# A causal mask moved into the free rows of a decay product, filled by GpSimd

## The chip, the core and the metric

One core of a Trainium2 chip. The metric is the time of one execution of the whole program in microseconds of device time: the median of three runs, and beside it one profiled execution. Throughout, TensorE runs at a granted clock of 1.00, its upper level of 2.4 GHz.

## What is computed

A block of a hybrid model over 512 tokens of width 1024 and a second block behind it. What matters here is the gated delta rule in the first block, in chunks. In the reference:

```python
G = jnp.cumsum(gc, axis=-1)
tri = jnp.tril(jnp.ones((C, C), dtype=bool))
strict = jnp.tril(jnp.ones((C, C), dtype=bool), -1)
gamma = jnp.exp(jnp.where(tri, G[..., :, None] - G[..., None, :], -jnp.inf))
kb = kc * bc[..., None]
A = jnp.where(strict, jnp.einsum("bnhid,bnhjd->bnhij", kb, kc) * gamma, 0.0)
T = lax.linalg.triangular_solve(A + eye, ...)
```

For each of 8 heads the keys' products with themselves are multiplied by decays that are 0 above the diagonal, and the triangular matrix that results is inverted. The kernel uses chunks of 128 tokens, four for each head.

## The kernel before

All weights come as panels of 128 output columns by 1024 (512 KB). SyncE loads a panel into one of two buffers (`conv_load`, L1289), ScalarE makes its rounded half (`split_hi`, L344), VectorE the rest (`split_lo`, L355), and TensorE forms 24 products of 128x512 with it (L552, L553, L555). Engines run their own lists of work, tied by semaphores. In this first stage each list goes through steps m, one panel each: panels 1 to 8 are keys, 9 to 16 queries, 17 to 24 values, 25 and on gates. ScalarE and VectorE split panel m + 2 in step m once they have caught up.

The decays of the keys. After panel 12 has its fourth slice, TensorE turns a small table of logarithms into 8 rows of 512 (`rows_turned(0)`), which ScalarE (`rows_hi`, L1530) and VectorE (`rows_lo`, L1534) write, as a rounded part and a rest, into partitions 0 to 7 and 32 to 39 of `rowsR`, row 0. The other 112 partitions hold zeros from a memset by GpSimd (L2966). `selR` (L1567, ScalarE, from `sel`, which VectorE forms at L1672 in its step m = 2) holds for each head ones in the two partitions of that head. In steps m = 12 to 15, two heads a step, TensorE spreads a head's row over 128 partitions (L1503), adds the causal mask by a second product, identity by `maskTb` in bf16 (L1504), and forms the keys' products (L1507). ScalarE takes the exponential with a bias for each row (L1617), VectorE multiplies the two (L1719) into `aA`. The queries' decays go the same way in steps 20 to 23 with `rowsR`, row 2, and their own masking product (L1477).

SyncE writes each head's `aA` to `scr_a` in DRAM (L1301, `g_a`), behind the loads of panels 16 and 18; behind the load of panel 19 it waits for all eight, reads the 32x32 blocks of the diagonal back (L1307, `d_u`) and goes on to panel 20. VectorE inverts these blocks in small steps between m = 18 and 26 (`solve`, L1273 and L1276). Behind panel 29 SyncE writes the inverse to `scr_t` (L1312, `d_w`), and reads it back head by head (L1325). From 218 us TensorE combines the blocks (`gdn_pe`, L1822 and on).

GpSimd's list in this stage is: memsets, part of the first norm and of the splitting of `x` (`first_pool`), the copies of the index keys (`key_copies`, L1446, for TensorE's L1489 behind panel 8), and then 13 times a transfer of 1 MB from DRAM to DRAM (`copy_quarter`, L928) and one that adds 1 MB to it (`add_sum`, L936), for weight sums that the feed-forward layers read hundreds of microseconds later. Sum i is issued when all moves before it have landed, and the next copy right behind it; before the eighth sum GpSimd also waits for `d_u`. Then come the level masks (`gdn_pool`, L1778), which wait for `d_w`.

Of the kernel before, what the change touches and what calls it, by code (L numbers as in the profile page):

```python
# [19 lines left out]
F32 = mybir.dt.float32  # L20
# [3 lines left out]
ACT = mybir.ActivationFunctionType  # L24
ALU = mybir.AluOpType
AX = mybir.AxisListType.X

P = 128
T = 512
NB = T // P  # L30
# [5 lines left out]
GH = 8  # L36
# [3 lines left out]
NEG = -1.0e30  # L40
# [79 lines left out]
for _name, _c in VEC:  # L120
# [2 lines left out]
NV = _n  # L123

MATS = ["ident", "ones", "lastrow", "blk64", "ropesel", "maskT", "zero0", "zero1", "zero2", "maskS", "hot",
        "lev5", "lev6"]
MO = {m: i for i, m in enumerate(MATS)}


# [35 lines left out]
def build(nc, I, out):  # L165
    with ExitStack() as ctx:
# [19 lines left out]
        identb, maskTb = (sb(n, [P, P], BF16) for n in ("identb", "maskTb"))  # L186
# [48 lines left out]
        def rep(ap, n):  # L235

            return ap.unsqueeze(1).broadcast_to([ap.shape[0], n, ap.shape[1]])
# [1197 lines left out]
        def first_pool(pool):  # L1435
            late_pool(pool, "norm1")
            for t in range(1, DT, 2):
                pool.wait_ge(n_hi, t + 1)
                pool.wait_ge(x_ready, t)
                pool.tensor_tensor(xl[:, t, :], x_scaled[:, t, :], xh[:, t, :].bitcast(F32), ALU.subtract).then_inc(x_ready, 1)  # L1440
# [8 lines left out]
        def conv_pe(pe):  # L1449
# [14 lines left out]
            for m in range(4, ZGA + ALONE):  # L1464
# [33 lines left out]
                if 12 <= m < 16:  # L1498
                    pe.wait_ge(g_rl, 1)
                    for s in range(2):  # L1500
                        hd, row, dots = 2 * (m - 12) + s, pb[4 + 2 * s][:, :], pb[5 + 2 * s]
                        wait(pe, g_e1, hd - 1)
                        pe.matmul(row, selR[:, hd, :], rowsR[:, 0, :], start=True, stop=False)  # L1503
                        pe.matmul(row, identb[:, :], rep(maskTb[:, :], NB), start=False, stop=True).then_inc(g_r1, 1)  # L1504
                        wait(pe, g_a, hd - 1)
                        for b in range(NB):
                            t = pe.matmul(dots[:, B(b)], kF[:, hd, B(b)], kF[:, hd, B(b)], start=True, stop=True)  # L1507
                        t.then_inc(g_kk, 1)
# [16 lines left out]
        sel = coef[:, 1, 0:GH]  # L1525

        def rows_hi(act, r):
            act.wait_ge(g_cr, 1 + r)
            act.wait_ge(s_set, 5)
            act.activation(rowsR[0:8, 2 * r, :], pb[6][0:8, :], ACT.Copy).then_inc(g_rh, 1)  # L1530

        def rows_lo(dve, r):
# [4 lines left out]
        def conv_act(act):  # L1537
            first_act(act)
            for m in range(2, ZGA + ALONE):
# [22 lines left out]
                if m == 4:  # L1562
                    act.wait_ge(s_mats, 32)
                    act.activation(identb[:, :], ident, ACT.Copy).then_inc(s_maskb, 1)
                    act.activation(maskTb[:, :], M("maskT"), ACT.Copy).then_inc(s_maskb, 1)
                    act.wait_ge(g_sel, 1)
                    act.activation(selR[:, :, :], sel.unsqueeze(2).broadcast_to([P, GH, P]), ACT.Copy).then_inc(g_sel, 1)  # L1567
                for c in {9: [4, 5], 10: [6, 7]}.get(m, TURN.get(m, [m - 3] if 11 <= m < 27 else [])):
                    hd, bank = c % 8, pb[2 + c % 2]
                    act.wait_ge(g_tr, c + 1)  # L1570
# [62 lines left out]
        def gate_dve(dve, n):  # L1633

            t, second = gate_tile(n)
            if second:
                dve.wait_ge(out_free, n + 1)
                dve.tensor_tensor(kF[:, t, :], kF[:, t, :], gtmp[t % 2], ALU.mult).then_inc(g_gm, 1)

        def conv_dve(dve):  # L1640
            first_dve(dve)
            for m in range(ZGA + ALONE):
# [71 lines left out]
                if 12 <= m < 16:  # L1714
                    for s in range(2):
                        hd = 2 * (m - 12) + s
                        dve.wait_ge(g_e1, hd + 1)
                        dve.wait_ge(g_kk, hd + 1)
                        dve.tensor_tensor(aA[:, hd, :], pb[5 + 2 * s][:, :], aA[:, hd, :], ALU.mult).then_inc(g_a, 1)  # L1719
                if 20 <= m < 24:  # L1720
                    for s in range(2):
                        hd = 2 * (m - 20) + s
# [1236 lines left out]
        def _(pool):  # L2959
# [2 lines left out]
            pool.memset(epsc[:, 1:2], 128.0 * EPS).then_inc(s_set, 1)  # L2962
            pool.memset(zeros, 0.0).then_inc(g_zero, 1)
            pool.memset(inv32, 0.0).then_inc(s_set, 1)
            for r in (0, 2):
                pool.memset(rowsR[:, r, :].bitcast(F32), 0.0).then_inc(s_set, 1)  # L2966
            pool.wait_ge(s_set, 3)
            pool.memset(yb[:, 2:4, :].rearrange("p a b -> p (a b)")[:, 0:1024:33], 1.0).then_inc(g_w0, 1)
            first_pool(pool)
            key_copies(pool)  # L2970
            copy_quarter(pool, 0, s_sums)
            for i in range(EARLY):
# [615 lines left out]
def _matrices():  # L3588
    i, j = np.arange(P)[:, None], np.arange(P)[None, :]
    out = np.zeros((P, len(MATS), P), np.float32)  # L3590
    out[:, MO["ident"]] = i == j
    out[:, MO["ones"]] = 1.0
    out[:, MO["lastrow"]] = (i == P - 1) * np.ones_like(j)
    out[:, MO["blk64"]] = (i // 64 == j // 64) / 64.0
    r = (j - 64) % 32
    out[:, MO["ropesel"]] = (j >= 64) & (i % 32 == r)
    out[:, MO["maskT"]] = np.where(j < i, NEG, 0.0)
    out[:, MO["maskS"]] = np.where(j > i, NEG, 0.0)
    out[:, MO["hot"]] = (i >= 64) & (i % 32 == j) & (j < 16)
    for l in (5, 6):  # L3600
        b = 1 << l
        out[:, MO[f"lev{l}"]] = (i // (2 * b) == j // (2 * b)) & (i // b % 2 == 0) & (j // b % 2 == 1)
    return out
# [102 lines left out]
```

## Time and profile before

| | us |
|---|---|
| median of three runs | 2117.58 (2115.51 to 2117.63) |
| profiled execution | 2118.94 |
| its span | 2117.1 |
| TensorE busy | 2096.8 (99%) |
| VectorE busy | 1495.1 (71%) |
| ScalarE busy | 1101.9 (52%) |
| GpSimd busy | 561.7 (27%) |

The profile's page gives the busy time of each engine and the costliest instructions; the views below it give waits, the chain of work that ended last, and each engine's instructions in order of time. TensorE's matmuls are pipelined: one lasts 0.39 us in the records, but the next starts 0.23 us after it. The stage of the change is the first 220 us.

### The profile page before, as it was taken

Reading aid. Unit: us, or ns where it says so; the run is one execution under the profiler, and the core shown is the slowest. Engines: PE = TensorE matmul, PEld = TensorE weight load, DVE = VectorE, ACT = ScalarE, POOL = GpSimd, SP = SyncE. Lnnn points to the kernel's source line nnn. Section 1 sums busy time; section 2 is a strip of 40 time slices with the busy share of each in tenths; the row PEclk is TensorE's granted clock in tenths of the full one; section 3 lists DMA queues with packets and bytes.
Section 4 is the critical chain, followed back from the end, with each engine's and each line's share of the span. In section 5 each row is a group of like instructions: output and inputs, shape, how many; then the busy total and the mean of one; then the engine's idle time right before and its main releaser. Section 6 shows DMA issues by size and latency. Waiting matters only on the chain.

```text
span 2117.1 us, 32333 instructions
## 1 busy us (share of the span) xinstructions
PE 2096.8 (99%) x12060; PEld 1821.4 (86%) x12060; DVE 1495.1 (71%) x2428; ACT 1101.9 (52%) x1928; POOL 561.7 (27%) x475
## 2 busy tenths in 40 slices
PE   9999999999999999999999999999999999999998
PEld 6887898888888889888887899999887778999897
DVE  6878334777467686876777687877566875868775
ACT  5877433435444354453776454554445764544543
POOL 2100531243333110153774231101322222311012
PEclk9999999999999999999999999999999999999999
DMA  7997212446676565644845559887653235555663
GB/s 258 247 262 204 94 59 70 152 167 210 236 202 179 152 185 169 157 122 129 298 164 173 140 195 260 259 258 230 159 157 89 79 91 153 170 189 180 209 190 129
DMA packets 148348, 372.01 MB, mean 176 GB/s; under 512 B 39008, under 2 KB 43360, under 8 KB 132832
## 3 DMA queue, kind: packets, MB, share of 16 engines
q1 hardware_dynamic: 129600, 241.49, 33.9%
q0 software_dynamic: 10448, 76.55, 17.2%
q10 hardware_dynamic: 8144, 51.91, 6.9%
q8 instruction: 96, 1.57, 0.3%
q14 instruction: 60, 0.49, 0.1%
HBM read 356.78 MB, written 132.64 MB: 231 GB/s over the span
## 4 chain that ended last, share of the span: by engine, by line
PE 87%; DVE 5%; ACT 2%; DMA 2%; issue 1%; DVEq 1%; POOLq 0%; SPq 0%; POOL 0%; ACTq 0%
PE bank L430 8%; PE bank L431 8%; PE bank L434 8%; PE bank L552 6%; PE bank L555 6%; PE bank L553 6%; PE bank L998 5%; PE bank L1002 5%; PE bank L1000 5%; PE bank L449 4%; PE bank L448 4%; PE bank L447 4%; PE bank L2538 2%; PE bank L1798 1%; PE bank L2566 1%
## 5 line engine op out<-in xcount | busy, mean ns | idle before, releaser
L344 ACT ACTIVATE b_wh<-b_raw 128x1024 fp32r<-128x1024 f32 (+1 forms) x312 | 321.8, 1034 | 533.0 <-PE bank L434 245.7
L355 DVE TENSOR_TENSOR b_wl<-b_raw,b_wh 128x1024 fp32r<-128x1024 f32 (+2 forms) x269 | 338.8, 1262 | 110.3 <-ACT b_wh L344 107.2
L552 PE MATMUL bank<-b_xh,b_wh 128*128 128x512 f32 x712 | 294.6, 414 | 0.6 <-DVE b_wl L355 0.6
L553 PE MATMUL bank<-b_xl,b_wh 128*128 128x512 f32 x712 | 278.2, 391 | 0.0
L555 PE MATMUL bank<-b_xh,b_wl 128*128 128x512 f32 x704 | 275.9, 392 | 0.0
L1206 POOL TENSOR_TENSOR b_yl<-b_arena,b_yh 128x512 fp32r<-128x512 f32 x42 | 65.2, 1553 | 537.3 <-ACT b_yh L1117 342.6
L430 PE MATMUL bank<-b_xh,b_wh 128*128 128x512 f32 x504 | 196.9, 391 | 0.0
L431 PE MATMUL bank<-b_xl,b_wh 128*128 128x512 f32 x504 | 196.1, 389 | 0.0
L434 PE MATMUL bank<-b_xh,b_wl 128*128 128x512 f32 x496 | 193.1, 389 | 0.0
L355 POOL TENSOR_TENSOR b_wl<-b_raw,b_wh 128x1024 fp32r<-128x1024 f32 (+1 forms) x45 | 103.9, 2310 | 226.1 <-ACT b_wh L344 188.4
L555 PEld LDWEIGHTS bank<-b_xh,b_wl 128*128 128x128 f32 x704 | 132.1, 188 | 29.1
L552 PEld LDWEIGHTS bank<-b_xh,b_wh 128*128 128x128 f32 x712 | 134.2, 188 | 24.9 <-DVE b_wl L355 1.3
L553 PEld LDWEIGHTS bank<-b_xl,b_wh 128*128 128x128 f32 x712 | 134.4, 189 | 21.2 <-issue 0.2
L998 PE MATMUL bank<-b_seven_hi,b_more_wh 128*128 128x256 f32 x512 | 145.0, 283 | 0.0
L1002 PE MATMUL bank<-b_seven_hi,b_more_wl 128*128 128x256 f32 x512 | 144.9, 283 | 0.0
L1000 PE MATMUL bank<-b_seven_lo,b_more_wh 128*128 128x256 f32 x512 | 144.9, 283 | 0.0
L355 DVE TENSOR_TENSOR b_more_wl<-b_more_raw,b_more_wh 128x1024 fp32r<-128x1024 f32 x92 | 120.0, 1305 | 32.1 <-ACT b_more_wh L344 29.8
L998 PE MATMUL bank<-b_seven_hi,b_wh 128*128 128x256 f32 x496 | 140.6, 283 | 0.4 <-DVE b_wl L355 0.4
L1000 PE MATMUL bank<-b_seven_lo,b_wh 128*128 128x256 f32 x496 | 140.4, 283 | 0.0
L1002 PE MATMUL bank<-b_seven_hi,b_wl 128*128 128x256 f32 x496 | 140.3, 283 | 0.0
L344 ACT ACTIVATE b_more_wh<-b_more_raw 128x1024 fp32r<-128x1024 f32 x92 | 96.4, 1053 | 46.5 <-PE bank L449 19.8
L430 PEld LDWEIGHTS bank<-b_xh,b_wh 128*128 128x128 f32 x504 | 94.6, 188 | 19.3
(576 smaller groups left out, 5539.8 us busy)
## 6 DMA issues: line engine op xcount, KB each, us to landing
scr_sums<-in_quarters POOLq DMA_DIRECT2D x37, 1024.0 KB, 9.8
scr_sums<-in_quarters ACTq DMA_DIRECT2D x35, 1024.0 KB, 5.2
b_raw<-scr_sums SPq DMA_DIRECT2D x110, 256.0 KB, 3.3
b_more_raw<-scr_sums SPq DMA_DIRECT2D x108, 256.0 KB, 3.2
scr_sums<-scr_sums POOLq DMA_DIRECT2D x24, 1024.0 KB, 8.5
b_raw<-in_quarters SPq DMA_DIRECT2D x92, 256.0 KB, 3.0
b_more_raw<-in_quarters SPq DMA_DIRECT2D x76, 256.0 KB, 3.1
scr_sums<-in_quarters ACTq DMA_DIRECT2D x8, 1536.0 KB, 8.8
```

Of the source, the lines that this page charges most:

```text
L344: act.activation(panel_hi_lo(n)[0][:, cols], raw_of(n)[:, cols], ACT.Copy).then_inc(w_hi, 1)
L355: dve.tensor_tensor(lo, raw_of(n)[:, cols], hi.bitcast(F32), ALU.subtract).then_inc(w_lo, 1)
L430: pe.matmul(bank[:, :], ph[:, w], hi[:, x, :], start=(k == 0), stop=False)
L431: last = pe.matmul(bank[:, :], ph[:, w], lo[:, x, :], start=False, stop=(n in SIDE_BY_SIDE and k == kt - 1))
L434: last = pe.matmul(bank[:, :], pl[:, w], hi[:, x, :], start=False, stop=(k == kt - 1))
L447: pe.matmul(bank, hi, ph, start=start, stop=False, skip_group_check=more)
L552: pe.matmul(bank[:, :], ph[:, w], hi[:, x, :], start=(k == 0), stop=False)
L553: last = pe.matmul(bank[:, :], ph[:, w], lo[:, x, :], start=False, stop=(n in SIDE_BY_SIDE and k == kt - 1))
L555: last = pe.matmul(bank[:, :], pl[:, w], hi[:, x, :], start=False, stop=(k == kt - 1))
L998: pe.matmul(bank, ph[:, w], xs_hi[i][:, k, :], start=(i < 4 and k == 0), stop=False, skip_group_check=(i > 3))
L1000: pe.matmul(bank, ph[:, w], xs_lo[i][:, k, :], start=False, stop=False, skip_group_check=(i > 3))
L1002: m = pe.matmul(bank, pl[:, w], xs_hi[i][:, k, :], start=False, stop=(k == 3), skip_group_check=(i > 3))
```

## The change

The mask goes into the first product. New constant matrices are loaded with the others: `barrier` holds, in each of the free 112 partitions but one, -1e30 in the columns before some place a, and `reach` ones from a on. Their product is -1e30 or less where a column lies before a row with a place between. The places are 1 to 127 without every eighth (4, 12, ...), as 111 fit; the entries that these leave unmasked lie beside the diagonal at the middle of a group of eight columns, and VectorE bounds the exponentials by 1e15 before it multiplies. GpSimd copies `barrier` into row 0 of `rowsR` (128x512, in place of a memset) and adds `reach` to the spread `sel` for `selR` (128x1024, in place of ScalarE's fill). Both stand behind `first_pool` and ahead of `key_copies`, behind a wait for the constants and one for `g_sel`, 1. ScalarE's `rows_hi` now waits for `g_sel`, 2.

```diff
-MATS = [..., "lev5", "lev6"]
+MATS = [..., "lev5", "lev6", "barrier", "reach"]
@@ conv_pe, 12 <= m < 16
-                        pe.matmul(row, selR[:, hd, :], rowsR[:, 0, :], start=True, stop=False)
-                        pe.matmul(row, identb[:, :], rep(maskTb[:, :], NB), start=False, stop=True).then_inc(g_r1, 1)
+                        pe.matmul(row, selR[:, hd, :], rowsR[:, 0, :], start=True, stop=True).then_inc(g_r1, 1)
@@ rows_hi
             act.wait_ge(s_set, 5)
+            act.wait_ge(g_sel, 2)
@@ conv_act, m == 4
-                    act.wait_ge(g_sel, 1)
-                    act.activation(selR[:, :, :], sel.unsqueeze(2).broadcast_to([P, GH, P]), ACT.Copy).then_inc(g_sel, 1)
@@ conv_dve, 12 <= m < 16
-                        dve.tensor_tensor(aA[:, hd, :], pb[5 + 2 * s][:, :], aA[:, hd, :], ALU.mult).then_inc(g_a, 1)
+                        dve.scalar_tensor_tensor(out=aA[:, hd, :], in0=aA[:, hd, :], scalar=GAMMA_MAX, in1=pb[5 + 2 * s][:, :],
+                                                 op0=ALU.min, op1=ALU.mult).then_inc(g_a, 1)
@@ gpsimd
-            for r in (0, 2):
-                pool.memset(rowsR[:, r, :].bitcast(F32), 0.0).then_inc(s_set, 1)
+            pool.memset(rowsR[:, 2, :].bitcast(F32), 0.0).then_inc(s_set, 1)
             ...
             first_pool(pool)
+            pool.wait_ge(s_mats, 32)
+            pool.wait_ge(g_sel, 1)
+            pool.tensor_copy(blk(rowsR[:, 0, :]), rep(M("barrier"), NB)).then_inc(s_set, 1)
+            pool.tensor_tensor(selR[:, :, :], bc(sel, P), rep(M("reach"), GH), ALU.add).then_inc(g_sel, 1)
             key_copies(pool)
@@ _matrices
+    free = [r for r in range(P) if not (r < GH or 32 <= r < 32 + GH)]
+    for r, a in zip(free, [a for a in range(1, P) if a % 8 != 4]):
+        out[r, MO["barrier"]] = NEG * (np.arange(P) < a)
+        out[r, MO["reach"]] = np.arange(P) >= a
```

## Rows read from the trace of the kernel before

**Rows 1.** Busy time by stretch: length, five engines, TensorE clock, DMA share, GB/s.

```profile
130.00:150.00 20.00, 20.00 (x98) 16.55 (x97) 14.15 (x21) 11.67 (x35) 2.68 (x4) 1.00 0.90 227
150.00:210.00 60.00, 57.46 (x294) 46.29 (x293) 53.34 (x103) 46.06 (x96) 4.84 (x7) 1.00 0.77 215
```

**Rows 2.** Waits of TensorE, 30 to 420 us: total us, times, longest us.

```profile
PE bank L1521 <- DVE b_arena L1735: 1.9, 3, 0.7
...
PE bank L1822 <- DMA b_arena<-scr_t: 0.2, 1, 0.2
```

**Rows 3.** Chain of waits in order of time: start us, us, what. Last masked pair.

```profile
119.62 0.23 PE bank L1503
119.85 0.23 PE bank L1504
```

**Rows 4.** Chain of waits, same columns: the transfer of panel 21.

```profile
136.77 8.89 DMA b_raw<-in_gv
```

**Rows 5.** VectorE L1719 and L1428: count, ns min/median/max, first and last start, shapes.

```profile
L1719 DVE TENSOR_TENSOR b_gdn_a<-bank,b_gdn_a x8: 690/692/693, 99.3 to 125.5; 128x512 f32<-128x512 f32 x8
L1428 DVE SCALAR_TENSOR_TENSOR b_arena<-b_h,b_arena,bank x8: 739/742/748, 21.4 to 28.5; 128x512 f32<-128x512 f32 x8
```

**Rows 6.** Order of ScalarE: start us, us, instruction, idle before and its releaser.

```profile
44.91 1.06 ACT L1567 ACTIVATE b_gdn_sel<-b_coef 128x1024 fp32r<-128x1024 f32 x1
46.38 1.06 ACT L344 ACTIVATE b_wh<-b_raw 128x1024 fp32r<-128x1024 f32 x1 [0.41 <-PE bank L555]
```

**Rows 7.** Order of VectorE: the row of `sel`.

```profile
44.72 0.16 DVE L1672 TENSOR_TENSOR b_coef<-b_mats 128x8 f32<-128x8 f32 x1
```

**Rows 8.** Order of GpSimd: key copies, first copy and first sum of quarters.

```profile
32.02 1.36 POOL L1446 COPY b_rrow<-b_arena 64x512 f32<-64x512 f32 x2 [0.45 <-DVE b_arena L1668]
34.04 0.76 POOL L928 DMA_DIRECT2D scr_sums<-in_quarters  x1 [0.66 <-issue]
40.05 0.88 POOL L936 DMA_DIRECT2D scr_sums<-in_quarters  x1 [5.25 <-DMA scr_sums<-in_quarters]
```

**Rows 9.** GpSimd L1778, a product with a repeated matrix (columns as rows 5).

```profile
L1778 POOL TENSOR_TENSOR b_arena<-b_gdn_a,b_mats x16: 1264/1282/2251, 213.3 to 300.1; 128x512 f32<-128x512 f32 x16
```

**Rows 10.** Order of GpSimd: seventh, eighth and thirteenth sum, then the level masks.

```profile
112.85 0.81 POOL L936 DMA_DIRECT2D scr_sums<-scr_sums  x1 [12.16 <-DMA scr_sums<-in_quarters]
...
134.97 0.81 POOL L936 DMA_DIRECT2D scr_sums<-scr_sums  x1 [20.77 <-DMA b_gdn_y<-scr_a]
...
197.87 0.81 POOL L936 DMA_DIRECT2D scr_sums<-in_quarters  x1 [9.56 <-DMA scr_sums<-in_quarters]
...
213.35 5.99 POOL L1778 TENSOR_TENSOR b_arena<-b_gdn_a,b_mats 128x512 f32<-128x512 f32 x4 [14.67 <-DMA scr_t<-b_gdn_y]
```

**Rows 11.** Order of SyncE's issues: blocks read back, then panels 20 and following.

```profile
129.68 2.34 SPq L1307 DMA_DIRECT2D b_gdn_y<-scr_a  x4
132.07 25.65 SPq L1289 DMA_DIRECT2D b_raw<-in_gv  x5
```

**Rows 12.** Writes to `scr_a` at 116 to 118 and 124.5 to 127 us, with landing.

```profile
L1301 SPq DMA_DIRECT2D scr_a<-b_gdn_a x2: 326/326/327, 116.5 to 117.6; - x2
DMA to landing us min/median/max: 9.0/9.1/9.2
...
L1301 SPq DMA_DIRECT2D scr_a<-b_gdn_a x2: 319/320/320, 125.2 to 126.2; - x2
DMA to landing us min/median/max: 2.0/2.7/3.5
```

**Rows 13.** Order of VectorE: split of panel 20, then the solver's first step.

```profile
141.46 1.21 DVE L355 TENSOR_TENSOR b_wl<-b_raw,b_wh 128x1024 fp32r<-128x1024 f32 x1
...
142.82 0.18 DVE L1273 TENSOR_TENSOR b_gdn_y<-b_gdn_y 128x31 f32<-128x31 f32 x1
```

**Rows 14.** Order of TensorE: first product of panel 20.

```profile
144.83 0.48 PE L552 MATMUL bank<-b_xh,b_wh 128*128 128x512 f32 x1
```

**Rows 15.** Writes to `scr_t`, with landing.

```profile
L1312 SPq DMA_DIRECT2D scr_t<-b_gdn_y x4: 326/590/620, 208.8 to 210.4; - x4
DMA to landing us min/median/max: 2.1/2.6/2.7
```

More of the change, by code:

```diff
@@ L125 @@
 MATS = ["ident", "ones", "lastrow", "blk64", "ropesel", "maskT", "zero0", "zero1", "zero2", "maskS", "hot",
-        "lev5", "lev6"]
+        "lev5", "lev6", "barrier", "reach"]
 MO = {m: i for i, m in enumerate(MATS)}
@@ L1638, in gate_dve @@
                 dve.tensor_tensor(kF[:, t, :], kF[:, t, :], gtmp[t % 2], ALU.mult).then_inc(g_gm, 1)
+        GAMMA_MAX = 1.0e15
         def conv_dve(dve):
```

## The prediction

> **What bounds the kernel now.** I read the busy time by stretch first. Between 130 and 150 us TensorE is busy all 20.00 us; between 150 and 210 us it is busy 57.46 of 60, and VectorE 53.34 [rows 1]. So before 150 us only TensorE's own work counts, and after it VectorE comes close to being the bound. The waits say the same: TensorE waits three times, 1.9 us in all, for VectorE's L1735, and once, 0.2 us, for the copy of `scr_t` [rows 2]. Then the chain of waits, followed in order of time: the products at 92 to 132 us stand on it one behind the other, and each of the eight masking products L1504 holds it for 0.23 us just as each L1503 does; the last pair is shown [rows 3]. From 132 us it goes through VectorE, a panel's transfer that took 8.89 us [rows 4], ScalarE, and then VectorE nearly alone to 208 us. The last view is the order of GpSimd's instructions and the time from issue to landing of the transfers beside them, because the change puts a wait into GpSimd's queue.
>
> **TensorE.** The change removes eight L1504 products, one a head. Each holds the chain for 0.23 us [rows 3]: 8 x 0.23 = 1.8 us, all in a stretch in which TensorE is the bound. L1503 stays, its free rows filled with the mask at no columns more. The whole saving is there by 119.9 us, where the last of them stands.
>
> **VectorE.** Eight L1719 multiplications become a minimum and a multiplication in one instruction. L1719 takes 692 ns; the same kind of instruction, one operand in PSUM, takes 742 ns at L1428 [rows 5]. 8 x 0.05 = 0.4 us. Before 130 us TensorE doesn't wait for this result (the product is read by SyncE and by later work), so I take 0, with 0.4 as the other end.
>
> **ScalarE.** The fill of `selR`, 1.06 us, goes. The next split started after 0.41 us of waiting for TensorE [rows 6]: it will only wait longer. Worth 0. The new wait in `rows_hi` is for a fill that ends 40 us earlier: 0.
>
> **GpSimd, the fills.** They stand after the first norm and before the key copies. They need `g_sel`, which VectorE raises at its L1672, at 44.72 us plus 0.16 [rows 7]. In the kernel before GpSimd was at the key copies by 32.02 us [rows 8]. The copy of the barrier rows is a 512-element copy as L1446 is, 1.36 us for two [rows 8], so 0.7; the upper end is L1778's 1.28 [rows 9]. The sum for `selR` is 1024 elements: twice L1778's 1282 ns [rows 9], 2.6 us; with nothing lower at hand than twice the 0.68 of a copy, the bounds are 1.4 and 2.6, and I take 2.4 as the kind of instruction is L1778's. The fills end near 44.9 + 0.7 + 2.4 = 48.0 (47.0 to 48.8). The key copies end 1.4 us later, near 49.4. TensorE wants them behind panel 8, while VectorE at 44.72 us is in its step m = 2, six steps earlier: 0. The memset that goes stood ahead of the norm, on an idle engine: 0. The constants grow by 128 KB; their first reader here is ScalarE just ahead of its 44.91, which shows no wait [rows 6]: 0.
>
> **GpSimd, what is queued behind the wait.** Behind it stand not only the key copies, but the transfers of `copy_quarter` and `add_sum`: 13 copies and 13 sums of 1 MB, each sum waiting for the moves before it. From the start of the key copies to the first issue it took 34.04 - 32.02 = 2.0 us [rows 8], so that issue comes at 50.0 instead of 34.04: 16 us later (15 to 16.8). The first sum then waited for the first copy until 40.05, 6.0 us. From the first sum at 40.05 to the seventh at 112.85 are six steps of 12.1 us [rows 8, 10]; the seventh moves to 56.0 + 72.8 = 128.8. Its partner, the copy issued 0.5 us later, needs about one step: it would end near 141 instead of 125.
>
> In the kernel before, that is the quiet stretch. GpSimd waits there, 20.77 us in all, for the blocks read from `scr_a`, and moves nothing from about 125 to 134.97 us [rows 10]. In it SyncE writes the last two heads to `scr_a`, reads the blocks back from 129.68 us, and behind these, in the same queue, issues the load of panel 20 at 132.07 [rows 11]. With GpSimd's transfers under way two writes to `scr_a` took 9.0 and 9.2 us; without them 2.0 and 3.5 [rows 12]. A loaded panel took 8.89 us [rows 4]. So the delayed chain meets just these.
>
> Here is what they may cost. The blocks are needed by the first L1273 at 142.82 - 1.8 = 141.0 [rows 13]. Issued from 127.9 to 130.2 (129.68 and 2.34 us of issuing, less 1.8) and landing like the loaded writes 9.1 us after the last issue, they land near 139.3: in time by 1.7 us. If the writes before them land late as well, by up to 9.2 - 3.5 = 5.7 us, they are 4 us late. Panel 20, issued at 132.07 - 1.8 = 130.3 and loaded, lands at 139.2; its two splits take 1.06 [rows 6] and about 1.2 us, so it is ready at 141.5. TensorE starts on it at 144.83 - 1.8 = 143.0 [rows 14]. Cover: 1.5 us; with the 5.7 of the writes ahead of it in the queue the cost is 4.2. The two delays run side by side and are not added. Bounds 0 and 4.2. The writes at 123.4 and 124.4 fall into the end of one GpSimd pair (116 to 128.5), so I take a third, 1.5 us. It can't be hidden after 150 us, where VectorE follows without a gap.
>
> The chain of sums then goes on: the eighth starts near 142 instead of 134.97, and the thirteenth, 62.9 us later [rows 10], at 205 instead of 197.87. Taking a step, it ends near 216. The inverse is written to `scr_t` from 208.80 us, four transfers landing 2.1 to 2.7 us after issue [rows 15]: now beside the last sum. By the ratio of [rows 12], 9.1 to 2.75, they would land 6 us later; the lower bound is 0, if the sum is through by then. TensorE has no cover there: it already waits for this copy at 218 us [rows 2], and so does GpSimd at 213.35 [rows 10]. I take 1.8, a third of the upper end: only one of GpSimd's transfers is left then, not a pair as in [rows 12].
>
> **The sum.** -1.8 (TensorE) + 0 + 0 + 1.5 (blocks and panel 20) + 1.8 (`scr_t`) = +1.5 us. The profiled execution took 2118.94 us, 2117.1 of it span: 2120.4. It is 1.4 us above the median of the runs shown, 2117.58, so against those the forecast is 2119.1.
>
> **The rivals**, on the scale of the median.
> 1. The saving is kept: the queues share the DMA engines in turn, and a short transfer beside a long one takes twice its time, not three times. Then the blocks land at 130.2 + 2 x 2.75 = 135.7, panel 20 no later than 139.2, both inside their cover, and the writes to `scr_t` lose 2.7 us at most, of which a last sum that ends early takes the rest. 2117.6 - 1.8 = 2115.8. For it: TensorE is busy all 20.00 us at 130 to 150 us, so nothing there is late now [rows 1]. Against it: the loaded writes took 9.1 us where the others took 2.75 [rows 12], and at 213 us there is no cover. The Trainium skill, DMA: Bandwidth & Descriptors, section "Queues, rings and completion order", has the rule behind this rival: each DMA engine goes round between the queues that have work, a packet from each. By that rule the time would be this rival's; the trace agrees that both queues move on side by side, but not with twice.
> 2. Slower. GpSimd's wait for `g_sel` sets the order of the transfers, and both meetings cost their upper ends: -1.8 + 4.2 + 6 = +8.4, 2126; it decides from the point at which the writes to `scr_a` end more than 1.5 us late, panel 20's cover. With one of them at its end, +4.2 to +5, 2122. For it: transfers fill 0.90 of the engines' time at 130 to 150 us [rows 1]. [...]
> 3. Faster than the saving. With GpSimd's transfers elsewhere the panel that took 8.89 us lands early, VectorE's run of work starts up to 0.9 us earlier (ScalarE split it at 136.77 + 8.89 = 145.7, while TensorE had left panel 19 by 144.83 [rows 4, 14]), and of the 1.9 us of waits behind it some go too: -1.8 - 0.9 to -1.8 - 1.9, about 2114.
> 4. The change does nothing for the end: VectorE's run from 150 us takes the 1.8 us back as waits of TensorE. It needs VectorE's run to start at its old time, which hangs on the panel of 8.89 us. 2117.6, inside the forecast's own range.
>
> **How the numbers follow.** The forecast and rival 4 hold 0.48 (2116.5 to 2121.8), rival 1 0.26, rival 2 0.21, rival 3 0.05. About 0.2%, 4.2 us, is what a measurement of this kernel can tell from no change. Faster by more than that needs rival 3 and more: 0.02. Slower by more is most of rival 2 and a little of the forecast: 0.22. The rest, 0.76, is the same. The range reaches from 2114.8 (rival 1 and a microsecond) to 2124.5 (half of rival 2).
>
> **What would show it.** Of the profile after: L1504 gone and TensorE's stretch at 92 to 127 us shorter by 1.8; GpSimd's first `copy_quarter` near 50 us; its seventh sum near 129, with no wait of 20 us behind it; the reads of `scr_a` landing after 137 instead of before 135; new or longer waits of TensorE at 143 to 165 (L552, L1515, L1521) and at L1822; the last sum near 205. If the seventh sum is near 113 as before, my reading of the wait is wrong, and everything after the first line falls with it. If the transfers move but the landings don't lengthen, rival 1 holds.

## The result and the profile after

| | before | after |
|---|---|---|
| median | 2116.89 us (2115.51 to 2117.63) | 2130.78 us (2127.62 to 2131.45) |
| ratio to before, 95% interval | | 1.0062 (1.0050 to 1.0073) |
| span of the profiled execution | 2117.1 us | 2128.9 us |

The kernel became slower: the medians lie 13.9 us apart, and the ratio is 1.0062. The forecast was 2119.1, 1.5 us over the kernel before, and its range ended at 2124.5. In the kernel after, some of the lines behind L1503 have moved by one or two: L1506 and on are the products of the keys, L1514 and L1520 stand for L1515 and L1521, L1779 for L1778, L1823 for L1822.

First the waits of TensorE, 100 to 260 us (us in total, times, the longest; those of 0.5 us and less are left out):

```profile
PE bank L1823 <- DMA b_arena<-scr_t: 7.1, 1, 7.1
PE bank L1454 <- ACT b_arena L1559: 4.8, 1, 4.8
PE bank L1460 <- DVE b_arena L1710: 1.8, 1, 1.8
PE bank L1520 <- DVE b_arena L1736: 1.2, 2, 0.7
```

In place of 1.9 + 0.2 us [rows 2] there are 14.9 us, and three of the waits are large: two at the turn to panel 20 and one at the copy of `scr_t`. The busy time by stretch (columns as rows 1) shows them with their clock, with the last stretch of the kernel before ahead of the three of the kernel after:

```profile
210.00:230.00 20.00, 19.47 (x117) 16.47 (x116) 8.35 (x7) 10.59 (x15) 15.23 (x11) 1.00 0.66 182
...
130.00:150.00 20.00, 13.40 (x59) 10.38 (x58) 8.85 (x15) 5.79 (x21) 1.35 (x2) 0.84 0.98 269
150.00:210.00 60.00, 58.03 (x297) 47.05 (x295) 54.26 (x98) 48.50 (x101) 6.72 (x10) 1.00 0.84 234
210.00:230.00 20.00, 12.92 (x58) 10.66 (x57) 6.97 (x12) 4.97 (x6) 6.66 (x5) 0.89 0.86 200
```

From 130 to 150 us TensorE was busy 20.00 of 20 us [rows 1], now 13.40; from 210 to 230 us it was busy 19.47, now 12.92. Between the two stretches nothing changed (58.03 of 60 against 57.46). The loss has two places, 75 us apart.

GpSimd's order shows the delay (start us, us, instruction, idle before and releaser; these columns hold for all orders below):

```profile
42.75 1.06 POOL L2972 CAST b_gdn_rows<-b_mats 128x512 fp32r<-128x512 f32 x1 [13.45 <-DVE b_coef L1672]
43.77 2.34 POOL L2973 TENSOR_TENSOR b_gdn_sel<-b_coef,b_mats 128x1024 fp32r<-128x1024 f32 x1
...
48.82 0.76 POOL L928 DMA_DIRECT2D scr_sums<-in_quarters  x1 [0.66 <-issue]
...
124.03 0.81 POOL L936 DMA_DIRECT2D scr_sums<-in_quarters  x1 [14.30 <-DMA scr_sums<-in_quarters]
...
137.39 0.81 POOL L936 DMA_DIRECT2D scr_sums<-scr_sums  x1 [12.02 <-DMA scr_sums<-in_quarters]
...
152.59 0.81 POOL L936 DMA_DIRECT2D scr_sums<-scr_sums  x1 [13.85 <-DMA scr_sums<-in_quarters]
...
212.31 0.81 POOL L936 DMA_DIRECT2D scr_sums<-in_quarters  x1 [10.39 <-DMA scr_sums<-in_quarters]
224.15 5.91 POOL L1779 TENSOR_TENSOR b_arena<-b_gdn_a,b_mats 128x512 f32<-128x512 f32 x4 [11.02 <-DMA scr_t<-b_gdn_y]
```

GpSimd idles 13.45 us for VectorE's `sel` and issues its first 1 MB copy at 48.82 instead of 34.04 us [rows 8]. The rows at 124.03, 137.39 and 152.59 are the sixth, seventh and eighth sum. The seventh stood at 112.85 before and the thirteenth at 197.87 [rows 10]; now they stand at 137.39 and 212.31. The quiet stretch before the eighth sum, 20.77 us of waiting for the blocks [rows 10], is gone: it now waits 13.85 us for its own chain.

SyncE's order has what the prediction did not foresee:

```profile
122.88 0.58 SPq L1289 DMA_DIRECT2D b_raw<-in_gv  x1
126.02 11.45 SPq L1307 DMA_DIRECT2D b_gdn_y<-scr_a  x4
137.52 23.87 SPq L1289 DMA_DIRECT2D b_raw<-in_gv  x5
...
212.50 9.11 SPq L1312 DMA_DIRECT2D scr_t<-b_gdn_y  x4
```

The four issues that read the blocks took SyncE 2.34 us [rows 11] and now take 11.45; the four writes of the inverse, which were begun from 208.8 to 210.4 us and took 0.62 us at most [rows 15], now take 9.11 in all. The single issues of the two lines (count, ns min/median/max, first and last start):

```profile
L1307 SPq DMA_DIRECT2D b_gdn_y<-scr_a x4: 322/1412/8171, 126.0 to 135.4; - x4
...
DMA to landing us min/median/max: 4.0/10.4/11.7
...
L1312 SPq DMA_DIRECT2D scr_t<-b_gdn_y x4: 326/590/7477, 212.5 to 214.1; - x4
...
DMA to landing us min/median/max: 2.5/9.4/9.8
```

So not only do the small transfers land late (10.4 and 9.4 us in the median). SyncE itself stands for 8.17 and 7.48 us at one issue, and what is queued behind it, panel 20 the first time, starts that much later. The chain of work that ended last shows it too (start us, us, what). It runs through the four issues at L1307, then through the load of panel 21, which SyncE issues right behind panel 20's, and at the second place through the last write of the inverse:

```profile
127.17 8.17 SPq L1307
...
135.38 2.09 SPq L1307
...
138.12 11.21 DMA b_raw<-in_gv
...
214.14 9.84 DMA scr_t<-b_gdn_y
```

ScalarE's order (a row of before first, then two of after) and TensorE's show the arrival:

```profile
138.38 1.06 ACT L344 ACTIVATE b_wh<-b_raw 128x1024 fp32r<-128x1024 f32 x1 [3.33 <-PE bank L555]
...
143.22 1.06 ACT L344 ACTIVATE b_wh<-b_raw 128x1024 fp32r<-128x1024 f32 x1 [12.28 <-DMA b_raw<-in_gv]
144.18 0.61 ACT L1559 ACTIVATE b_arena<-b_arena 128x512 f32<-128x512 f32 x1
```

```profile
144.85 1.11 PE L1454 MATMUL bank<-b_mats,b_arena 128*128 128x128 f32 x4 [4.78 <-ACT b_arena L1559]
147.78 1.02 PE L1460 MATMUL bank<-b_mats,b_arena 128*8 128x128 f32 x4 [1.82 <-DVE b_arena L1710]
148.45 0.78 PE L552 MATMUL bank<-b_xh,b_wh 128*128 128x512 f32 x1
...
150.89 0.40 PE L552 MATMUL bank<-b_xh,b_wh 128*128 128x512 f32 x1
...
228.57 1.94 PE L1823 MATMUL bank<-b_mats,b_arena 128*128 128x128 f32 x8 [7.08 <-DMA b_arena<-scr_t]
```

ScalarE had the split of panel 20 (L344) at 138.38 before, after 3.33 us of waiting for TensorE. Now it waits 12.28 us for the transfer, and L1559, which TensorE's L1454 needs, stands behind it in the same list. After the pause the same product L552 takes 0.78 us and 2.4 us later 0.40 again: the granted clock of 140 to 150 us is 0.69 in the mean, the lower of the two levels, 1.2 GHz, in a part of it. TensorE had been idle for 4.78 us before that. Behind the second wait the pattern repeats (0.78 at 230.16, and 0.78 is also the clock of 220 to 230 us).

**Where 13.9 us come from.** TensorE starts on panel 2 at 23.60 us in the profile of before and at 20.8 to 23.5 in the others, also where the code up to there is the same (20.80 in e2, 21.89 in e7). So I count each event of TensorE from there. The turn to panel 19 is the start of the four small products L1454 ahead of it. The third row is the first L1515 (now L1514), which stands behind the products of panel 20; below I call it step 20. All columns are of one profiled execution each.

| us after the start of panel 2 | before | after | difference |
|---|---|---|---|
| turn to panel 19 | 114.53 | 112.67 | -1.86 |
| L1515 (now L1514) of step 20 | 127.34 | 134.01 | +6.67 |
| start of L1822 (now L1823) | 194.40 | 207.24 | +12.84 |
| the rest, to the end of the span | 2093.50 | 2107.57 | +14.07 |

To panel 19 the saving is there in full. From there to step 20, over the turn to panel 20, 8.5 us are lost: 4.78 + 1.82 of waits, the rest the lower clock and what follows. The second meeting shows its whole wait, 7.08 against 0.17, less 0.7 us that the stretch between gave back; another 1.2 us go behind it, where the clock is at the lower level again.

### The profile page after: what moved, and what is told of

It reads as the page before. It is cut to its first block, busy times and chain, and to the rows that moved or that the text cites. A ratio compares the mean times of both kernels' runs of the same rounds, so it can differ in the third digit from the quotient of the medians.

```text
span 2128.9 us, 32318 instructions
## 1 busy us (share of the span) xinstructions
PE 2098.2 (99%) x12052; PEld 1823.1 (86%) x12052; DVE 1495.9 (70%) x2428; ACT 1101.3 (52%) x1927; POOL 567.3 (27%) x476
## 4 chain that ended last, share of the span: by engine, by line
PE 87%; DVE 5%; ACT 3%; DMA 2%; issue 1%; DVEq 1%; SPq 1%; POOLq 0%; POOL 0%; ACTq 0%
PE bank L430 8%; PE bank L431 8%; PE bank L434 8%; PE bank L552 6%; PE bank L555 6%; PE bank L553 6%; PE bank L998 5%; PE bank L1000 5%; PE bank L1002 5%; PE bank L449 4%; PE bank L448 4%; PE bank L447 4%; PE bank L2539 2%; PE bank L1799 1%; PE bank L2567 1%
## 5 line engine op out<-in xcount | busy, mean ns | idle before, releaser
L344 ACT ACTIVATE b_wh<-b_raw 128x1024 fp32r<-128x1024 f32 (+1 forms) x312 | 321.8, 1034 | 556.0 <-PE bank L434 231.3
L552 PE MATMUL bank<-b_xh,b_wh 128*128 128x512 f32 x712 | 295.7, 415 | 0.7 <-DVE b_wl L355 0.6
L552 PEld LDWEIGHTS bank<-b_xh,b_wh 128*128 128x128 f32 x712 | 134.7, 189 | 25.1 <-DVE b_wl L355 1.3
L344 ACT ACTIVATE b_more_wh<-b_more_raw 128x1024 fp32r<-128x1024 f32 x92 | 96.4, 1054 | 44.7 <-PE bank L449 19.8
```

The costliest lines, as they stand in the source:

```text
L344: act.activation(panel_hi_lo(n)[0][:, cols], raw_of(n)[:, cols], ACT.Copy).then_inc(w_hi, 1)
L552: pe.matmul(bank[:, :], ph[:, w], hi[:, x, :], start=(k == 0), stop=False)
```

## The experiments

The theory: GpSimd's 1 MB transfers, 15 us late, are in flight while SyncE issues its small ones for `scr_a` and `scr_t`; they hold up SyncE's issuing, and all three large waits follow. The rivals: the new instructions cost something themselves (the fills, the minimum), the late start costs in another way and the meeting is only a companion, or the saving of 1.8 us doesn't exist. The edits below are against the kernel after, where nothing else is said. "First meeting" is L1307 with the two waits at panel 20, "second meeting" is L1312 with the wait at L1823.

**e1, the fills between the first sums.** GpSimd does all it did, but sends its first copy and first sum off before it waits for `sel`.

```diff
-            pool.wait_ge(s_mats, 32)
-            pool.wait_ge(g_sel, 1)
-            pool.tensor_copy(blk(rowsR[:, 0, :]), rep(M("barrier"), NB)).then_inc(s_set, 1)
-            pool.tensor_tensor(selR[:, :, :], bc(sel, P), rep(M("reach"), GH), ALU.add).then_inc(g_sel, 1)
...
             for i in range(EARLY):
+                if i == 1:
+                    pool.wait_ge(s_mats, 32)
+                    pool.wait_ge(g_sel, 1)
+                    pool.tensor_copy(...)
+                    pool.tensor_tensor(...)
```

> The changed kernel, but GpSimd's wait for g_sel and its two fills stand between the first and the second sum of the quarters, where it waits some 10 us for a transfer anyway. Theory (the harm is only that the transfers behind the wait start 15 us late): the first copy is issued near 34 us again, the eighth sum waits about 20 us for the blocks, SyncE's four issues of the blocks take 2.3 us together and not 11.5, and the saving of the eight products is left: 1.8 us faster than the kernel before, about 2115. Rival (the fills, the larger constants or the two-step operation on VectorE cost the time): it stays near 2131.

Measured: 2114.19 us beside 2117.85 for before, ratio 0.9987 (0.9978 to 0.9996). The first copy is issued at 31.59 us, the issues at L1307 and the landings are:

```profile
L1307 SPq DMA_DIRECT2D b_gdn_y<-scr_a x4: 322/566/778, 128.4 to 130.2; - x4
...
DMA to landing us min/median/max: 2.4/2.9/3.0
```

No issue is held (0.78 us at most), L1312 takes 2.26 us, and TensorE's large waits are gone (L1823 0.7 us in all). The products, the minimum and the fills are all there, and the whole loss is gone. So the loss lies in the place of the wait and the fills, and none of it in what the new instructions cost.

**e2, the wait alone.** The kernel before, with the two waits and nothing else of the change.

```diff
             first_pool(pool)
+            pool.wait_ge(s_mats, 32)
+            pool.wait_ge(g_sel, 1)
             key_copies(pool)
```

> The kernel before with one addition: GpSimd waits for the constants and for g_sel ahead of the key copies; no fill, no new matrix, all products kept. Theory: the whole loss without the saving, 13.9 + 1.8 = 15.7 us slower than the kernel before, near 2132.6; the waits of TensorE behind step m = 17 (about 6.6 us) and at the copy of scr_t (about 7) are there. The fills of 3.4 us are missing from the delay (12.6 us instead of 16), so one of the two meetings may be weaker. Rival: no change against before.

Measured: 2125.84 us, ratio 1.0043 (1.0030 to 1.0055), 8.0 us over before and half of the 15.7 expected. GpSimd's order, SyncE's order and the waits of TensorE:

```profile
42.29 2.00 POOL L1446 COPY b_rrow<-b_arena 64x512 f32<-64x512 f32 x2 [13.51 <-DVE b_coef L1672]
...
127.75 0.81 POOL L936 DMA_DIRECT2D scr_sums<-scr_sums  x1 [13.07 <-DMA scr_sums<-in_quarters]
```

```profile
128.61 9.93 SPq L1307 DMA_DIRECT2D b_gdn_y<-scr_a  x4
```

```profile
PE bank L1454 <- ACT b_arena L1559: 3.3, 1, 3.3
PE bank L1460 <- DVE b_arena L1710: 2.3, 1, 2.3
PE bank L1822 <- DMA b_arena<-scr_t: 1.3, 1, 1.3
```

The first meeting comes with the wait: a pair is issued at 127.75, a microsecond before SyncE's reads, one of which is held for 6.63 us. The second does not come. The first copy goes out at 44.95 instead of 48.82 us, the steps between the sums are 12.7 us long instead of 13.1, and the last sum stands at 202.76 instead of 212.31; L1312 follows at 213.31, 10.5 us behind it, and takes 2.25 us. The wait alone makes some 8 us. That the fills behind it bring the second meeting on top fits this, but no run changes their time alone.

**e3, the pause one sum earlier.** GpSimd's wait for the blocks, which stands ahead of the eighth sum, is put ahead of the seventh.

```diff
-EARLY, FIRST_EARLY = 13, 7
+EARLY, FIRST_EARLY = 13, 6
```

> The changed kernel with GpSimd's wait for the blocks moved one sum forward (ahead of the seventh instead of the eighth), so that the late chain is quiet again while the blocks are read. Theory: SyncE's issues of the blocks take about 2.3 to 4 us, TensorE's waits of 4.8 and 1.8 us near 142 to 148 us and its slow clock behind them go, 8 us are won back; the wait at the copy of scr_t stays or grows, as the last sum is still late (near 206): about 2122. Rival (it is bandwidth over the whole stretch, not this meeting): under 3 us won.

Measured: 2128.57 us, ratio 1.0056 (1.0040 to 1.0071). The meeting was not kept away. The sixth sum, at 125.06 us, was the one that met the reads; L1307 took 9.67 us, one issue 6.24. I had counted the sums by the steps of 12.1 us of before, and they are longer here. The second meeting had another form: L1312 took 3.23 us at 209.84, its writes landing in 3.0 to 3.9 us, but the last sum at 213.00 came ahead of the reads of `scr_t`, and L1823 still waited 5.1 us. The run says only that a pause behind the meeting does not help.

**e4, the pauses at both places.** As e3, and the last sum waits for the inverse's writes (`d_w`).

```diff
+                if i == EARLY - 1:
+                    pool.wait_ge(d_w, 16 * NB)
```

> As the one before, and the thirteenth sum also waits until the inverse is written to scr_t. Theory: both meetings are gone though the transfers are still late: TensorE's wait for the copy of scr_t falls from 7.1 us to under 1, and the time is that of the saving alone, about 2115 to 2117. Rival (the late transfers cost through something else): over 2122.

Measured: 2128.81 us, ratio 1.0060 (1.0047 to 1.0072). Here L1307 was clean (2.43 us at 134.06), but not by the edit: up to the last sum this is the program of e3. In e3's execution the panel's load issued at 106.28 us landed after 5.6 us; in this one, the load issued at 106.33, behind a pair of 105.60, took 13.83 us. ScalarE, the last heads' `aA` and the blocks all came later; step 20 came 130.73 us after the start of panel 2, only 3.3 us earlier than in the kernel after. Which transfers meet can thus differ between executions of one program, and a profile shows one of them. The last sum, now at 215.53, stood in front of the reads of `scr_t` and a panel's load, and TensorE got a new wait:

```profile
PE bank L1842 <- ACT b_gdn_y L1894: 5.5, 1, 5.5
PE bank L1454 <- ACT b_h L1559: 2.4, 2, 1.3
PE bank L552 <- DVE b_wl L355: 1.6, 2, 1.5
```

L1823 now waits 1.3 us in all, but what that gains goes again behind it. The cost was moved, not removed, and the run says nothing of the time without meetings.

**e5, panel 20 ahead of the blocks.** SyncE reads the blocks behind panel 20's load, not ahead of it.

```diff
-                if n == 19:
+                if n == 20:
```

> The changed kernel, but SyncE issues the load of panel 20 ahead of reading the blocks back, so that it no longer stands behind their issues. Theory A (what hurts at 142 us is that the panel is stuck in SyncE's queue behind an issue that itself takes 8 us): TensorE's wait of 4.8 us behind step m = 19 goes, the blocks still land late (near 145) and hold VectorE's solver some 3 us; 3 to 6 us faster than the changed kernel. Theory B (bandwidth: the panel is as late wherever it is issued): within 1 us of it, 2130.8.

Measured: 2126.19 us, ratio 1.0037 (1.0024 to 1.0051). L1307 takes 11.93 us all the same, two of its issues 4.23 and 5.64. Panel 20's load, now issued at 126.97 us ahead of them, lands after 10.7 us, and the wait of 4.8 us at its turn is gone; of the other, at L1460, 1.6 us stay. What stands behind the held issues is late instead: panel 21's load is issued at 139.39 and takes 8.85 us, and TensorE waits 3.0 us at L1454 one turn later, 1.5 at L1514, and 5.4 at L1823. Against the kernel after some 5 us come back by the ratios (1.0037 against 1.0062) and 3.4 us in the profiles, so panel 20's place in the queue was a part of the price, and no more than a part.

**e6, half the delay.** The key copies and the first copy of a quarter go ahead of the wait; the first sum still stands behind the fills.

```diff
+            key_copies(pool)
+            copy_quarter(pool, 0, s_sums)
             pool.wait_ge(s_mats, 32)
...
-            key_copies(pool)
-            copy_quarter(pool, 0, s_sums)
```

> The changed kernel with the key copies and the first copy of quarters ahead of GpSimd's wait and fills: the first sum comes near 48 instead of 55.7 (before: 40.1), half of the delay. Theory (each meeting is a matter of phase): the seventh sum's partner ends near 133, so the blocks meet only its tail, and the last sum ends near 210, so scr_t meets its tail; 2 to 8 us slower than before, 2119 to 2125. Rival (any delay costs the same): 2131. Rival (bandwidth in proportion): +7, 2124.

Measured: 2121.51 us, ratio 1.0017 (1.0007 to 1.0026). The first sum is at 45.80 us, between 40.05 [rows 8] and 55.67. The first meeting is there (L1307 10.89 us, one issue 7.40; waits of 3.8 and 2.3 us at panel 20); the second is not (the last sum at 201.57, L1312 2.25 us at 212.46, L1823 1.2 us). Two kernels with the first meeting alone, e2 and e6, are slower than before by 8 and by 3.5 us. With the product's 1.8 us, which only e6 saves, the price of this meeting is 8 and 5.3 us. In the profiles, counted at step 20, it is 8.1 us (e2 over before) and 8.9 us (e6 over e1). The profiled execution of e6 took 2123.64 us, and its ten executions 2119.16 to 2123.85: the others may have met in part only, which no profile shows.

**e7, the masking product twice.** The kernel before with L1504 issued twice; the second one adds the same mask again, which changes nothing in the exponential.

```diff
                         pe.matmul(row, identb[:, :], rep(maskTb[:, :], NB), start=False, ...)
+                        pe.matmul(row, identb[:, :], rep(maskTb[:, :], NB), start=False, stop=False)
```

> The kernel before with each of the eight masking products done twice (the mask counts double, which changes no result). Theory (TensorE's own work is the bound at 92 to 127 us, and VectorE's run behind it moves with it): 8 x 0.23 = 1.8 us slower. Rival (VectorE's run from 150 us has a start of its own and swallows it): 0.

Measured: 2118.51 us beside 2118.02, ratio 1.0001 (0.9993 to 1.0010). In the profile step 20 comes 2.0 us later, and the rest from panel 2 on is 1.5 us longer. 1.8 us are 0.08%, inside that interval; the timed runs alone can't tell them from nothing.

**e8, the pause ahead of the sixth sum.** What e3 had meant to do, with the sums counted from the profile.

```diff
-EARLY, FIRST_EARLY = 13, 7
+EARLY, FIRST_EARLY = 13, 5
```

> The changed kernel, with the existing pause of GpSimd for the panel's blocks put ahead of the sixth sum, the one that met the blocks' reads in the changed kernel, instead of ahead of the eighth. Theory (GpSimd's 1 MB pairs hold up SyncE's issues of the small transfers): the four issues at L1307 take some 2.4 us instead of 11.45, the waits of TensorE of 4.8 and 1.8 us at the turn to panel 20 go, and that turn comes back to some 125.5 us after the start of panel 2. The sums behind it all come later, so that the last pairs meet the Y-writes at L1312 in full: a wait of 5 to 8 us at L1823 stays or grows, and the whole is 2122 to 2128. Rival (the delay of the fills costs by another way, the meeting is only a companion): the waits at the turn to panel 20 stay though L1307 is clean.

Measured: 2129.37 us, ratio 1.0052 (1.0037 to 1.0068). GpSimd's order, SyncE's order, and the waits of TensorE of 100 to 260 us:

```profile
130.88 0.81 POOL L936 DMA_DIRECT2D scr_sums<-in_quarters  x1 [22.13 <-DMA b_gdn_y<-scr_a]
...
203.00 0.81 POOL L936 DMA_DIRECT2D scr_sums<-scr_sums  x1 [11.08 <-DMA scr_sums<-in_quarters]
...
215.01 0.81 POOL L936 DMA_DIRECT2D scr_sums<-in_quarters  x1 [10.66 <-DMA scr_sums<-in_quarters]
```

```profile
124.90 3.82 SPq L1307 DMA_DIRECT2D b_gdn_y<-scr_a  x4
...
206.66 8.35 SPq L1312 DMA_DIRECT2D scr_t<-b_gdn_y  x4
```

```profile
PE bank L1823 <- DMA b_arena<-scr_t: 11.5, 1, 11.5
PE bank L1520 <- DVE b_arena L1736: 2.3, 3, 1.1
```

The first meeting is gone. The pause is back (22.13 us), L1307 takes 3.82 us, its longest issue 1.79, the waits of 4.8 and 1.8 us don't exist, and step 20 is 125.98 us after the start of panel 2 instead of 134.01 (e1: 125.36). What was gained there is lost at the second meeting, which now has a full pair in flight, from 203.00 on, and one issue of 6.54 us: one wait of 11.5 us instead of 7.1, with the clock of 210 to 230 us at 0.66. The time was expected at 2122 to 2128 and came 1 us over.

**e9, no meeting, with GpSimd as late as in the kernel after.** As e8, and the sums 11 to 13 stand behind the panels' last power in GpSimd's list, after the second meeting's place.

```diff
-EARLY, FIRST_EARLY = 13, 7
+EARLY, FIRST_EARLY = 13, 5
@@ index_pool
+            for i in range(EARLY - 3, EARLY):
+                add_sum(pool, i)
+                if i < EARLY - 1:
+                    copy_quarter(pool, i + 1, s_sums)
@@ gpsimd
-            for i in range(EARLY):
+            for i in range(EARLY - 3):
```

> As e8, and only the first ten sums in the early loop; the sums 11 to 13 with their copies stand behind the panels' last power on GpSimd, after the Y-writes and their reads. The fills stay where the changed kernel has them, so GpSimd's transfers start 16 us late as there, but no pair meets one of SyncE's small transfers. Theory: both waits go (L1307 2.4 us, L1312 2.3 us, L1823 below 1.5 us) and the masking product's 1.8 us are kept: 2114 to 2117. Rival 1 (a late start of the transfers costs by itself): 2120 or more with L1307 and L1312 clean. Rival 2 (the three sums behind the power meet something else, the panels' own loads or vectors): clean at both places, a new wait of TensorE after the last power, 2118 to 2125.

Measured: 2116.95 us beside 2118.27, ratio 0.9991 (0.9982 to 1.0000). The wait, the fills and the first copy at 48.77 us are those of the kernel after. SyncE's order and TensorE's waits:

```profile
126.54 2.90 SPq L1307 DMA_DIRECT2D b_gdn_y<-scr_a  x4
...
206.52 2.25 SPq L1312 DMA_DIRECT2D scr_t<-b_gdn_y  x4
```

```profile
PE bank L1520 <- DVE b_arena L1736: 2.4, 3, 1.2
PE bank L1514 <- DVE b_gdn_rows L1534: 1.5, 1, 1.5
PE bank L1823 <- DMA b_arena<-scr_t: 1.4, 1, 1.4
```

This is the run that separates the theory from the rival of a late start: GpSimd's transfers start as late as in the kernel after, and the time is not longer than before. The edit moves the pause and three sums with their copies; the meetings are gone, and with them 14 us. It also thins the transfers of the stretch (the DMA share of 150 to 210 us is 0.73 instead of 0.84), but in e1 that share is 0.84 too, and nothing is lost. The time is at the upper end of what was expected; the profiled execution keeps 1.5 and 1.4 us of small waits that e11 doesn't have.

**e10 and e11, with and without the masking product, where nothing meets.** e11 is the code of e1 again; e10 is the same with L1504 put back.

```diff
-                        pe.matmul(row, selR[:, hd, :], rowsR[:, 0, :], start=True, stop=True).then_inc(g_r1, 1)
+                        pe.matmul(row, selR[:, hd, :], rowsR[:, 0, :], start=True, stop=False)
+                        pe.matmul(row, identb[:, :], rep(maskTb[:, :], NB), start=False, stop=True).then_inc(g_r1, 1)
```

> As e1 (the fills between the first sums, so that no pair meets the blocks), but the decays' key mask is added by the second product again, as in the kernel before: the mask stands in the free partitions too and the second product is issued besides. What is measured is the product alone, against e11. Theory: eight products on TensorE's path at 0.23 us, so 1.8 us over e11: about 2116.0, within 0.1% of the kernel before. Rival (the product was hidden, and e1's gain came from elsewhere): equal to e11 within 0.4 us.

> The same code as e1, again, on the chip and beside the runs of e9 and e10, for a difference of 2 us needs them side by side. Expected 2114.2 and a ratio of 0.9982 to 0.9992 to the kernel before; the first meeting absent (L1307 2.4 us, L1312 2.3 us). Rival: e1's 2114.2 was the chip's, and the ratio here holds 1.

Measured: e10 2117.13 us, ratio 0.9996 (0.9987 to 1.0005); e11 2116.55 us, ratio 0.9991 (0.9982 to 1.0000); before 2118.27. The medians are 0.6 us apart and the single runs of each scatter over 5 to 7 us, so the timed runs don't settle 1.8 us. The profiles do, up to the place where it arises: step 20 comes 127.14 us after the start of panel 2 with the product and 125.34 without, 1.80 us apart; to the end of the span it is 2.3 us. e11 repeats e1 in its mechanism (L1307 3.47 us, L1312 2.26, L1823 0.5). Its median is 2.4 us above e1's 2114.19, on another chip where before is 0.4 us above. What e1 gains over the kernel before is therefore 0.1%, 1.7 to 3.7 us by the two pairs of medians, with both intervals at 1.0000 or below.

## Why the prediction was wrong

**TensorE, -1.8: right.** The turn to panel 19 came 1.86 us earlier, and e10 against e11 gives 1.80.

**VectorE and ScalarE, 0: right.** L1719 with the minimum takes 687 ns, not 742: less than the 692 before [rows 5]. The upper end of 0.4 us came from another line's 742 ns and did not apply.

**The fills: right, a little early.** 1.06 and 2.34 us where 0.7 and 2.4 stood; they end at 46.1 instead of 48.0, since this execution began 2.3 us earlier. The first copy is at 48.82, forecast 50.0.

**The step between the sums: mis-sized.** I carried the 12.1 us of before over. From the first sum, 55.67, to the seventh, 137.39, the steps are 13.6 us. The seventh came 8.6 us after its forecast 128.8, though this execution began 2.3 us earlier, so it was the sixth pair that met the reads. That a pair would be in flight was right, which pair was not; and the quiet stretch was lost, as forecast.

**The blocks and panel 20, +1.5, with 4.2 as the bound: this step failed.** The measured price is 8.5 us. The step took the issues at their old 2.34 us [rows 11] and let only the landing grow. It took landings of 9.1 us for the blocks, and three of the four measured 10.1 to 11.7, so that half was sound; no wait for the blocks shows. But the issuing took 11.45 us, of which one transfer 8.17, and panel 20 stands behind it in the queue. Less the 2.3 us by which this execution began earlier, its issue was forecast at 128.0 and its landing at 136.9. It was issued at 137.52, 9.5 us later, and landed 5.7 us after that, not 8.9, at 143.2. That is 6.3 us late; less the cover of 1.5 us, 4.8 are left, which is TensorE's wait at L1454. "The two delays run side by side" was wrong with it: the queue puts one behind the other. Panel 21 followed, landing 11.21 us after its issue. Two things came on top that the step didn't have: ScalarE's list, in which L1559 stands behind the split, and the clock at its lower level after the pause.

**`scr_t`, +1.8, with 6 as the bound: mis-sized.** L1823 waits 7.08 us, and from step 20 on 6.2 us are lost up to it and 1.2 behind it. Here the wait goes by the landings: the last three of the four writes landed 9.0 to 9.8 us after their start, two of them though their issue was not held. That is the upper end (9.1), and I had taken a third. The reason for the third, that a single transfer loads less than a pair, does not hold here: the last sum, issued at 212.31 with nothing behind it, was enough to hold one of the issues at 212.5 to 214.1 for 7.48 us.

**The rivals.** Rival 2 is nearest to what happened: it named the wait and both meetings. Its point was the writes to `scr_a` ending late, which they did not: the last landed after 3.5 us, as before. Its sum, +8.4 us, was too low by 5.5: 4.3 of it at the first meeting (8.5 instead of 4.2), the rest at the second. Rival 1 would have brought the blocks in at 135.7. The last landed at 139.4, and more to the point the delay lay ahead of the landing. The rule that the Trainium skill (DMA: Bandwidth & Descriptors, section "Queues, rings and completion order") has for it speaks of packets of queues that have work. The 8.17 us lie in SyncE's own instruction, and no run here shows what it waited for. The saving that the rival names shows only in e1, e9 and e11, where nothing meets, and there as 1.3 to 3.7 us.

The range was too narrow for the same reason. The trace of before has no case of this meeting, and 4.2 and 6 us were ends made from landings alone, not bounds. That a third of each was taken was a judgement (of 6 us it would be 2.0, not 1.8), and no row gives it.

**When an issue is held.** The runs agree on the time that lies between a 1 MB transfer of GpSimd and SyncE's small ones. At L1307 GpSimd's sum was issued 0.9 to 2.7 us earlier in each run with a held issue (after 124.03 and 126.02, e2, e3, e5, e6), at L1312 0.2 us (after) and 3.7 us (e8). Where it was issued 10 us earlier, as at L1312 in e3 and e5 (199.88 and 200.69, against 209.84 and 211.40), no issue took more than 1.3 us. With no transfer of GpSimd in flight the longest at L1307 was still 1.3 to 1.8 us in e8, e9 and e11. In e3 and e5 the loss of 5 us behind L1312 has another place: the last sum, at 213.00 and 213.63, came before the reads of `scr_t` or among the writes, one of which, issued right behind it, landed after 8.5 us in e5 though its issue took 0.62. And the writes of L1301, which met pairs in every run, were not held: 0.32 to 0.33 us each, one of 0.96 in e7 apart, though they landed after up to 10.7. L1307 and L1312 move blocks of 32x32, 128 KB each time in rows of 128 bytes; L1301 moves 256 KB in rows of 512 bytes or more. That the many short rows make the difference is a guess, since no run changed them. It stays open, as does what the held issue waits for.

## What to carry to other kernels

Where an engine's list also issues transfers, a wait put into it moves all of them. Look for what each then meets, and don't count only the instruction that waits. In SyncE's queue price two things for a meeting, the issuing and the landing, and let everything behind the held issue slip by the first. And try the same edit one place later in the list before it is judged: here four lines moved past one copy and one sum turned 0.6% slower into 0.1% faster.

## What the runs showed of the hardware

- An issue by SyncE of one small transfer (a fourth of the blocks or of the inverse, 128 KB) took 0.32 to 0.78 us with GpSimd's queue quiet in before, e1, e4 and e10, and up to 0.97 in e7 and 1.8 in e8, e9 and e11. Of four that followed one of its 1 MB transfers within 4 us, one took 5.6 to 8.2 us (8.17 and 7.48 in the kernel after, 6.63 in e2, 6.24 in e3, 5.64 in e5, 7.40 in e6, 6.54 in e8).
- The held issue was the third of the four, and the fourth at L1312 in the kernel after; the others took up to 2.3 us, but in e5 the second took 4.23. Behind a transfer that was issued 10 us earlier the longest took 1.1 and 1.3 us.
- TensorE's clock was at its lower level after idle times of 4.78 and 7.08 us: the same product took 0.78 us, then 0.63, then 0.40, over some 2.4 us.
- A minimum and a multiplication in one VectorE instruction, with the second operand in PSUM, took 687 ns; the multiplication alone had taken 692.
